# Experts' weight tiles of 2 MB instead of 1 MB in a one-core transformer kernel

## The reference

```python
def expert_choice_moe(h, w_router, w_gate, w_up, w_down):
    cap = EC_CAPACITY_FACTOR * length // N_EXPERTS          # 2 * 256 // 16 = 32 rows
    aff = jax.nn.softmax((h @ w_router).astype(jnp.float32), axis=-1)
    gate, idx = lax.top_k(jnp.swapaxes(aff, 1, 2), cap)
    xe = h[bidx, idx]
    hid = jax.nn.silu(jnp.einsum("becd,edf->becf", xe, w_gate)) * jnp.einsum("becd,edf->becf", xe, w_up)
    ye = jnp.einsum("becf,efd->becd", hid, w_down) * gate[..., None].astype(h.dtype)
    return jnp.zeros_like(h).at[bidx, idx].add(ye)
```

## Time and profile before

| | us |
|---|---|
| median of 3 runs | 1912.13 (1910.47 to 1912.84) |
| the profiled execution | 1913.96 |
| its span | 1912.2 |

### The profile page before, as it was taken

One profiled execution on the slowest core, in us unless ns is written; L12 is line 12 of the kernel. 1 busy time (PEld: TensorE's weight loads), 2 busy tenths in 40 slices (PEclk: granted clock), 3 DMA queues, 4 the chain that ended last, 5 costly groups with the idle time before them and its releaser, 6 DMA issues.

```text
span 1912.2 us, 28670 instructions
## 1 busy us (share of the span) xinstructions
PE 1730.6 (91%) x11874; PEld 1378.2 (72%) x11879; DVE 822.0 (43%) x1160; ACT 675.8 (35%) x978; POOL 10.7 (1%) x8
## 2 busy tenths in 40 slices
PE   6999999899999999999999999998998776776666
PEld 6999987899999999768999965876785331221211
DVE  4555697755565556124655513732422111101111
ACT  4444556644454444123444323415503221111111
POOL 0000010000000000000000000000000000000000
PEclk9999999899999999999999999999998888778777
DMA  9555555355555554543555452322169999999997
GB/s 305 194 175 181 162 186 192 117 198 176 184 157 187 188 184 139 161 145 114 186 189 186 152 184 76 118 72 69 64 261 384 382 421 422 422 422 422 422 421 313
DMA packets 198853, 427.12 MB, mean 223 GB/s; under 512 B 9139, under 2 KB 146661, under 8 KB 174212
## 3 DMA queue, kind: packets, MB, share of 16 engines
q1 hardware_dynamic: 198788, 426.19, 61.7%
HBM read 425.12 MB, written 1.05 MB: 223 GB/s over the span
## 4 chain that ended last, share of the span: by engine, by line
PE 76%; DMA 13%; DVE 4%; ACT 3%; SPq 3%; issue 1%; DVEq 0%; ACTq 0%
PE banks L604 14%; PE banks L606 14%; PE banks L605 14%; DMA ring<-in_w_exp_up 11%; PE banks L1206 5%; PE banks L954 4%; PE banks L930 3%; PE banks L754 2%; SPq L546 2%; PE banks L706 1%; PE banks L1085 1%; PE banks L935 1%; DMA arena<-in_w_exp_down 1%; PE banks L1119 1%; PE banks L798 1%; PE banks L631 1%
## 5 line engine op out<-in xcount | busy, mean ns | idle before, releaser
L604 PE MATMUL banks<-x_split,w_split 128*128 128x256 f32 x1600 | 457.9, 286 | 19.1 <-DVE x_split L1821 9.7
L605 PE MATMUL banks<-x_split,w_split 128*128 128x256 f32 x1600 | 455.2, 284 | 0.0
L606 PE MATMUL banks<-x_split,w_split 128*128 128x256 f32 x1600 | 455.1, 284 | 0.0
L1804 DVE TENSOR_TENSOR w_split<-ring,w_split 128x1024 fp32r<-128x1024 f32 x288 | 346.6, 1224 | 247.7 <-ACT w_split L1314 247.3
L1314 ACT ACTIVATE w_split<-ring 128x1024 fp32r<-128x1024 f32 x288 | 296.1, 1051 | 199.4 <-PE banks L606 190.8
L604 PEld LDWEIGHTS banks<-x_split,w_split 128*128 128x128 f32 x1600 | 309.7, 194 | 22.9 <-issue 15.5
L605 PEld LDWEIGHTS banks<-x_split,w_split 128*128 128x128 f32 x1600 | 309.7, 194 | 0.1
L606 PEld LDWEIGHTS banks<-x_split,w_split 128*128 128x128 f32 x1600 | 309.6, 194 | 0.0
L604 PE MATMUL banks<-hid_split,w_split 128*128 128x256 f32 x704 | 199.6, 284 | 0.0
L605 PE MATMUL banks<-hid_split,w_split 128*128 128x256 f32 x704 | 199.2, 283 | 0.0
L606 PE MATMUL banks<-hid_split,w_split 128*128 128x256 f32 x704 | 199.2, 283 | 0.0
(11 more groups left out here) (364 smaller groups left out, 1880.2 us busy)
## 6 DMA issues: line engine op xcount, KB each, us to landing
ring<-in_ffn_w SPq DMA_DIRECT2D x132, 1024.0 KB, 5.3
arena<-in_w_exp_gate SPq DMA_DIRECT2D x58, 1024.0 KB, 24.6
ring<-in_w_exp_up SPq DMA_DIRECT2D x47, 1024.0 KB, 26.1
ring<-in_w_exp_down SPq DMA_DIRECT2D x45, 1024.0 KB, 24.5
ring<-in_w_mod SPq DMA_DIRECT2D x24, 1024.0 KB, 5.2
ring<-in_w_in SPq DMA_DIRECT2D x21, 1024.0 KB, 5.3
arena<-in_w_exp_down SPq DMA_DIRECT2D x19, 1024.0 KB, 26.5
arena<-in_w_exp_up SPq DMA_DIRECT2D x16, 1024.0 KB, 25.9
```

The lines of the kernel that those rows point to most:

```text
L604: mm(out_, hi, moving(0), start=start, stop=False, **kw)
L605: mm(out_, hi, moving(1), start=False, stop=False, **kw)
L606: return mm(out_, lo, moving(0), start=False, stop=stop, **kw)
L1804: ins = dve.tensor_tensor(half_part(n, o, 1), half_slot(n, o, columns), half_part(n, o, 0).bitcast(F32), ALU.subtract)
```

## The change

The experts' tiles become 2 MB: 512 rows of a matrix, four neighbouring rows or 16384 bytes to a partition (`k=4`), so six tiles for an expert. The buffers are used in pairs: three pairs of ring slots, three pairs in `ahead`, and as extra buffers `once` and `squares` whole; `gated` is no longer used. Sixteen MB can be loaded before the first expert starts, 17 before. The list of SP begins with the wait for `merged_ready`, then three pairs go to `ahead`, and then pairs of the ring alternate with the two extra ones. `reused_load` waits until both halves of a pair have been used. The PE waits for a tile's landing at each even product only and takes the halves of a pair by `half_of_pair`. What read every second column now reads every fourth, and the gains are dealt out by 16 matmuls of 32 columns by 4 in place of 4 of 64 columns by 8.

```diff
-        EXP_SLOTS = SLOTS + AHEAD
-        REUSED = 12 * (EXPERTS - 1) - EXTRA
+        PAIRS_E = 6
+        EXP_PAIRS = (SLOTS + AHEAD) // 2
+        REUSED = PAIRS_E * (EXPERTS - 1) - EXTRA
+        PAIR_0 = FIRST["experts"] + FIRST["experts"] % 2
...
-            exp_tiles = [w[0].rearrange("e (j p k) c -> j e p (k c)", p=P, k=2)[j]
-                         for w in (w_exp_gate_2, w_exp_up_2, w_exp_down_2) for j in range(4)]
+            exp_tiles = [w[0].rearrange("e (j p k) c -> j e p (k c)", p=P, k=4)[j]
+                         for w in (w_exp_gate_2, w_exp_up_2, w_exp_down_2) for j in range(2)]
...
-                q, s = u % EXP_SLOTS, (u + EXTRA) % 12
-                used = u + 1 if u < EXP_SLOTS else u - EXP_SLOTS + 12 + EXTRA + 1
-                sp.wait_ge(slot_free, FIRST["experts"] + used + (0 if more is None else 12 * more))
+                q, s = u % EXP_PAIRS, (u + EXTRA) % PAIRS_E
+                used = u + 1 if u < EXP_PAIRS else u - EXP_PAIRS + PAIRS_E + EXTRA + 1
+                sp.wait_ge(slot_free, FIRST["experts"] + 2 * used + (0 if more is None else 12 * more))
...
-            for s in range(2):
-                wait_free(sp, FIRST["experts"] + s)
+            def ring_free(q):
+                sp.wait_ge(slot_free, min(PAIR_0 + 2 * q - SLOTS + 2, FIRST["experts"]))
+
+            sp.wait_ge(sem("merged_ready"), 2)
+            for s in range(SLOTS // 2, EXP_PAIRS):
                 first_load(s)
-            sp.wait_ge(sem("merged_ready"), 2)
-            for s in range(SLOTS, SLOTS + AHEAD):
+            for s in range(SLOTS // 2):
+                ring_free(s)
                 first_load(s)
-            for s in range(2, SLOTS):
-                wait_free(sp, FIRST["experts"] + s)
-                first_load(s)
-                for b in ((0, 1, 2), (3, 4), (), ())[s - 2]:
-                    expert_load(extra[b], b, 1, sem("extra_in"))
+                if s < EXTRA:
+                    expert_load(extra[s], s, 1, sem("extra_in"))
...
-            for i in range(2):
-                for r in range(2):
-                    last = mm(ps[64 * r:64 * r + 64, 7, KD * i:KD * i + KD],
-                              ident.rearrange("p (c i) -> p i c", i=2)[:, i, :], gain_mod[:, 2:4, r:KD:2],
+            for i in range(4):
+                for r in range(4):
+                    last = mm(ps[32 * r:32 * r + 32, 7, 4 * i:4 * i + 4],
+                              ident.rearrange("p (c i) -> p i c", i=4)[:, i, :], gain_mod[:, 2:4, r:KD:4],
...
+            def half_of_pair(view, s):
+                return view[:, SLOT * (s % 2):SLOT * (s % 2) + SLOT]
+
             def take_first(s):
-                pe.wait_ge(*expert_full(s))
-                return expert_view(s)
+                if s % 2 == 0:
+                    pe.wait_ge(*expert_full(s // 2))
+                return half_of_pair(expert_view(s // 2), s)
```

More of the change, by code:

```diff
@@ L358, in build @@
         squares_flat = squares[:, :, :].rearrange("p k t -> p (k t)")
-        extra = [gated[:, :, :].rearrange("p a c -> p (a c)"), once[:, 0, :], once[:, 1, :],
-                 squares_flat[:, 0:SLOT], squares_flat[:, SLOT:2 * SLOT]]
+        extra = [once.rearrange("p a c -> p (a c)"), squares_flat]
         EXTRA = len(extra)
-        EXP_SLOTS = SLOTS + AHEAD
-        REUSED = 12 * (EXPERTS - 1) - EXTRA
+        PAIRS_E = 6
+        EXP_PAIRS = (SLOTS + AHEAD) // 2
+        REUSED = PAIRS_E * (EXPERTS - 1) - EXTRA
+        PAIR_0 = FIRST["experts"] + FIRST["experts"] % 2
+        assert SLOTS % 2 == 0 and AHEAD % 2 == 0
         assert r4.at <= ARENA
@@ L402, in expert_view @@
         def expert_view(q):
-            return slot(FIRST["experts"] + q) if q < SLOTS else ahead[:, q - SLOTS, :]
+            if q < SLOTS // 2:
+                i = (PAIR_0 + 2 * q) % SLOTS
+                return ring[:, i:i + 2, :].rearrange("p a c -> p (a c)")
+            return ahead[:, 2 * q - SLOTS:2 * q - SLOTS + 2, :].rearrange("p a c -> p (a c)")
         def expert_full(q):
-            if q < SLOTS:
-                n = FIRST["experts"] + q
+            if q < SLOTS // 2:
+                n = PAIR_0 + 2 * q
                 return slot_full[n % SLOTS], 16 * (n // SLOTS + 1)
-            return sem(f"ahead_{q - SLOTS}"), 16
+            return sem(f"ahead_{q - SLOTS // 2}"), 16
         w_ffn = [(ffn1_w1[0], ffn1_w3[0], ffn1_w2[0]), (ffn2_w1[0], ffn2_w3[0], ffn2_w2[0]),
@@ L551, in reused_load @@
             def reused_load(u, more=None):
-                q, s = u % EXP_SLOTS, (u + EXTRA) % 12
-                used = u + 1 if u < EXP_SLOTS else u - EXP_SLOTS + 12 + EXTRA + 1
-                sp.wait_ge(slot_free, FIRST["experts"] + used + (0 if more is None else 12 * more))
-                expert_load(expert_view(q), s, 1 + (u + EXTRA) // 12, expert_full(q)[0], more)
-            for s in range(2):
-                wait_free(sp, FIRST["experts"] + s)
+                q, s = u % EXP_PAIRS, (u + EXTRA) % PAIRS_E
+                used = u + 1 if u < EXP_PAIRS else u - EXP_PAIRS + PAIRS_E + EXTRA + 1
+                sp.wait_ge(slot_free, FIRST["experts"] + 2 * used + (0 if more is None else 12 * more))
+                expert_load(expert_view(q), s, 1 + (u + EXTRA) // PAIRS_E, expert_full(q)[0], more)
+            def ring_free(q):
+                sp.wait_ge(slot_free, min(PAIR_0 + 2 * q - SLOTS + 2, FIRST["experts"]))
+            sp.wait_ge(sem("merged_ready"), 2)
+            for s in range(SLOTS // 2, EXP_PAIRS):
                 first_load(s)
-            sp.wait_ge(sem("merged_ready"), 2)
-            for s in range(SLOTS, SLOTS + AHEAD):
+            for s in range(SLOTS // 2):
+                ring_free(s)
                 first_load(s)
-            for s in range(2, SLOTS):
-                wait_free(sp, FIRST["experts"] + s)
-                first_load(s)
-                for b in ((0, 1, 2), (3, 4), (), ())[s - 2]:
-                    expert_load(extra[b], b, 1, sem("extra_in"))
+                if s < EXTRA:
+                    expert_load(extra[s], s, 1, sem("extra_in"))
             sp.wait_ge(sem("h_seeded"), TT)
             sp.dma_start(gain_row, final_norm_g_2.partition_broadcast(P)).then_inc(sem("gain_row_in"), 16)
-            for u in range(EXP_SLOTS):
+            for u in range(EXP_PAIRS):
                 reused_load(u)
-            with sp.Fori(0, REUSED // EXP_SLOTS - 1) as i:
-                for u in range(EXP_SLOTS, 2 * EXP_SLOTS):
+            with sp.Fori(0, REUSED // EXP_PAIRS - 1) as i:
+                for u in range(EXP_PAIRS, 2 * EXP_PAIRS):
                     reused_load(u, i)
-            for u in range(REUSED // EXP_SLOTS * EXP_SLOTS, REUSED):
+            for u in range(REUSED // EXP_PAIRS * EXP_PAIRS, REUSED):
                 reused_load(u)
@@ L1170, in gather @@
                 for t in range(TT):
-                    w = tok[:, t, :].rearrange("p (j c i) -> p j i c", j=KD // 2, i=2)[:, k // 2, k % 2, :]
+                    w = tok[:, t, :].rearrange("p (j c i) -> p j i c", j=KD // 4, i=4)[:, k // 4, k % 4, :]
                     last = mm(o, w, picks[:, t, first:first + GROUP, :], start=(t == 0), stop=(t == TT - 1))
@@ L1228, in expert @@
                 for c in range(4):
-                    w = hid_e[0:64, :].rearrange("p (j c i) -> p j i c", j=2, i=2)[:, c // 2, c % 2, :]
+                    w = hid_e[0:64, :].rearrange("p (c i) -> p i c", i=4)[:, c, :]
                     last = mm(ps[:, 7, 64 * c:64 * c + 64], w, ident[0:64, 0:64],
@@ L1249, in expert, with take_later @@
                     last.then_inc(sem("spread_free"), 1)
+            def half_of_pair(view, s):
+                return view[:, SLOT * (s % 2):SLOT * (s % 2) + SLOT]
             def take_first(s):
-                pe.wait_ge(*expert_full(s))
-                return expert_view(s)
+                if s % 2 == 0:
+                    pe.wait_ge(*expert_full(s // 2))
+                return half_of_pair(expert_view(s // 2), s)
+            def take_later(s, more, e):
+                if e == 1 and s < 2 * EXTRA:
+                    if s == 0:
+                        pe.wait_ge(sem("extra_in"), 16 * EXTRA)
+                    return half_of_pair(extra[s // 2], s)
+                u = PAIRS_E * (e - 1) + s // 2 - EXTRA
+                if s % 2 == 0:
+                    full, first = expert_full(u % EXP_PAIRS)
+                    pe.wait_ge(full, first + 16 * (u // EXP_PAIRS + 1) + 16 * more)
+                return half_of_pair(expert_view(u % EXP_PAIRS), s)
             pe.wait_ge(sem("pick_ready"), 1)
@@ L1258, in _ @@
             expert(0, 0, take_first, 0)
[L1260 to L1268, removed]
             for e in range(1, GROUP):
@@ L1657, in _ @@
             act.wait_ge(sem("pe_mark"), PE_MARK["gains_paired"])
-            fn(pair_gain.rearrange("p a (j i) -> p a j i", i=2),
-               ps[:, 7, 0:2 * KD].rearrange("p (i a j) -> p a j i", i=2, a=2), ACT.Copy)
+            fn(pair_gain.rearrange("p a (j i) -> p a j i", i=4),
```

(1 more changed line is left out.)

## The result

The changed kernel takes 1926.88 us in the median of 4 runs (1925.65 to 1929.54); the kernel before took 1912.49 beside it. The ratio is 1.0078, 95% interval 1.0066 to 1.0090: 14.4 us slower, where I had forecast 1913.3 and a range up to 1919.0. The profiled execution took 1925.65, with a span of 1923.8. The two profiled spans are 11.6 us apart and not 14.4: the execution profiled before was 1.83 us above its median, this one 1.23 under.

The account below looks back on a forecast made before the run. From the fifth expert on the weight stream was taken as the bound. The data's end 0.5 us earlier put the last up pair 0.45 earlier; with 1.7 more in the tail, +1.2 us gave 1913.3, range 1906.5 to 1919.

Parts of the forecast that it names:

- four-column steps in place of two-column ones in gather and turning: PE weight loads in the experts: costed at nothing, or up to twice the time if the step did cost.
- the rival built on it: Weight loads with the four-column step take twice the time: +3.2 us at the restart, 1916 to 1918; chance 0.06.
- The rate of the stream: Expert weight loads in 16384-byte pieces: 2.472 us a MB, 0.013 less than before, about 424 GB/s.
- The first slope: Cost of piece length, 37.7 ns a KB from 1 to 2 KB; continued to 16 KB it gives 428 GB/s.
- the first rival: Per-piece cost goes on shrinking as between 1 and 2 KB: 2.449 us a MB, 4.0 us less, 1909.3; chance 0.17.
- The nearest row: The last slope, 38.5 ns a KB from 4 to 8 KB pieces, next to which 2.472 us a MB was taken.
- The start: Restart of the weight stream at the first expert waits for both halves of a pair: data at 1460.2, 3.0 us later.
- The idle time that gives it back: Stream idle in the first experts shrinks from 4.6 to 0.9 us, so 3.7 of 5.5 us come back.
- The tail: After the last up pair lands: two products instead of one, +1.7 us, with the pair taken 0.45 us earlier.
- Cut pieces: Rival: pieces are cut at 8192 bytes, the rate stays at 422 GB/s, 2.3 us more, 1915.6; chance 0.15.
- slower memory: Rival: memory likes longer pieces less; a 10% loss would give 44 us more, 1957; chance 0.07.
- The rival with the full clock in the tail: Clearly faster stream, 2.460 us a MB, and last products at full clock, 0.85 for 1.7 us: 3.0 less; chance 0.10.

Follow-up runs that it names:

- e4_two_pieces: The change's 2 MB transfers and buffer pairs, but each partition takes two pieces of 8192 bytes and all steps are of two columns: 1915.97 us, ratio 1.0016.
- e1_step2: The changed kernel with the gather of token rows reading every second column, as before the change: 1912.70 us, ratio 1.0000.
- f5_both_dealt: The changed kernel with token rows dealt out by ScalarE and hidden rows by VectorE, leaving no four-column step on the PE: 1909.56 us, ratio 0.9982.

## Why the prediction was wrong

**The step that failed** is the sentence of the tail paragraph in which I cost "four-column steps in place of two-column ones in gather and turning ... at nothing". The bound beside it, "up to twice", was right, and the rival built on it had the cause. But I priced it on the 24 records ahead of the second product alone, 3.2 us, and wrote "in part not given back" where I should have counted. The gathers in the second, third and fourth expert, 32 records each, lie in the stretch of which the same prediction says that the PE is the slower one there; 7.7 for 4.0 us is 11 us more for the three, and with 3.7 in the first the sum is the 14.4 us of the lines view. A bound of twice on 128 records of 17.1 us would have put the upper end of the range at 1930. With it fell the premise that an expert takes the PE about 25 us against 29.7 of the stream: it was 33.3 and 31.1 against 29.3. I took the value at the end of "nothing" because the row nearest to it showed no cost of a step of two, not because a row excluded one of four.

A page did state the rule. The Trainium skill (SBUF — State Buffer, Door 1: The DMA port swizzle) says that SBUF is read in lines of 16 bytes and that two accesses to a line are needed for full rate. With fp32 a step of two still has two, a step of four has one, and 3 lines hold 4 elements at step three. By the rule alone that is 1, 1.5, 2 and 2 times; the measured 1, 1.4, 1.9 and 1.9 agree to within 5%. Its next sentence, that fp32 may be strided by 4 for free, is what the runs contradict: 1.94 us for eight loads in place of 1.02. This holds at the full clock; at the half clock the turning's eight loads took 1.94 us for 1.78.

**The rate of the stream** was too low: I took 2.472 us a MB, the profile has 429 GB/s or 2.444. The first slope, 37.7 ns a KB, came close (2.449), so the first rival was right on its term; it is 0.028 x 176 = 4.9 us in favour of the change. The nearest row misled: I read a shrinking gain as a saturating rate. e4_two_pieces shows that the length of the piece does it. The 2.0 us a transfer that the prediction quotes from the Trainium skill (DMA: Bandwidth & Descriptors, Anatomy of one DMA — SWDGE (gpsimd) path) are stated there for transfers issued by GpSimd. Here SP issues them, and half the transfers brought no gain in rate in e4_two_pieces.

**The start** was right in its form. The restart hangs on the second half of a pair. In e1_step2, with the old step in the gather, the first reused load goes out at 1458.41 against my 1458.6, though 0.5 us of that is a later start of the whole part; in the change at 1461.23, by the gather. The gain matmuls cost less than the 0.85 us that I set: 0.67 for 0.41 us, 0.26 more.

**The idle time that gives it back** shrank where its premise held: 0.9 us forecast, 2.0 in e1_step2, of the 4.6 before. In the change it is 12.2. With these the end of the data can be summed again for the change: 1461.23 + 1.6 + 176 x 2.444 + 12.2 = 1905.2, and the last window with data, 1904 to 1908, has 193 GB/s, which ends it at 1905.8; before it was 1897.3.

```profile
1904.00:1908.00 4.00, 3.53 (x16) 2.06 (x20) 0.00 (x0) 0.38 (x1) 0.00 (x0) 0.56 0.45 193
```

**The tail** is 3.1 us longer in the change (11.6 of the span less 8.5 of the data's end), forecast 1.7. The timeline of the last expert, beside the earlier trace rows, splits it:

```profile
1898.26 3.31 PE L1212 MATMUL banks<-ring,arena 128*32 128x512 f32 x16 [1.78 <-DMA ring<-in_w_exp_up]
...
1903.72 2.12 PE L1236 MATMUL banks<-consts,arena 64*128 64x64 f32 x8 [2.16 <-DVE arena L2391]
...
1914.59 3.67 PE L1250 MATMUL banks<-arena 32*128 32x512 f32 x8 [2.16 <-DVE arena L2395]
```

The two products behind the last up landing take 3.31 us for the 1.93 of one, 1.4 more, near the 1.7 of the forecast, mostly at the half clock. (At the full clock one more is 0.86 us: two take 1.92 in f5_both_dealt.) The turning's step adds 0.2 there, since it took 1.97 us before, at the half clock too. The down products add 0.4, and the last up pair is taken 0.4 nearer to the end of the data. The last 0.8 follow from the matmuls onto the token rows, 3.67 us where they took 1.99, at a granted clock of 0.53 for 1.00. So the term was right in kind, and what came on top of it is mainly the clock.

**The sum** from the forecast to the measurement: 4.9 us less by the rate, 2.6 more by the start, 11.3 more by the idle time and 1.4 more by the tail are 10.4, which makes 1923.7. The other 3 us are the distances of the two profiled executions from their medians.

**The other rivals.** Cut pieces and slower memory are out: 429 GB/s in pieces of 16384 bytes. The rival with the full clock in the tail was right on the rate alone. One reading of the earlier trace rows was also off: the 421 or 422 GB/s end at slice 38, and slice 39 has 313; nothing in the sum hangs on it.

## What to carry to other kernels

A layout that makes a transfer's pieces longer also moves the elements that the PE reads: find every operand whose step changes, and count all its instructions, each in the stretch in which it stands. Where an engine sets the pace for a while, a cost on it passes through the buffers to the stream behind them, even when the stream is the bound of the rest. Deal the columns out once, in a copy that is made anyway, rather than in each weight load.

## What the hardware showed that I had not expected

At the full clock eight loads of 128 x 128 fp32 weights took 1.02 us from every second column, 1.47 from every third, 1.94 from every fourth and 1.98 from every eighth. Loads of 64 rows from every fourth column took the same 1.94 us for eight at granted clocks of 1.00 and 0.50, where those from every second took 1.02 and 1.78. VectorE's product of 64 x 512 fp32 took 1027 ns for 683 when it was written at a step of 128 columns, its inputs read in order. ScalarE's copy of 1024 columns from PSUM, read at a step of four and written in order, stayed at 1114. And pieces of 16384 bytes still gain over 8192: 385, 408, 418, 422 and 429 GB/s from 1 to 16 KB. The length is not all, since another stretch of 1 KB pieces has 348.
